# Hybrid mLSTM / MLA / PEER layer: the dots' second operand in PSUM, two product banks, and every second u block split on GpSimd

## Chip, cores and metric

One core of one Trainium2 chip runs the whole layer. The metric is the device time of one execution in microseconds (us). The kernel before takes 1566.36 us, the median of 3 runs (1564.87 to 1568.07).

## The reference, cut to what matters

S = 512 tokens, D = 1024. A mixer (mLSTM heads and latent attention) comes first, then a normalisation, then the sparse block, PEER, which this change is about:

```python
def peer(h, w_q, keys_1, keys_2, u_table, v_table):   # tables: 16384 experts x 1024
    def block(xb):                                    # 128 tokens
        qry = (xb @ w_q).reshape(TB, PEER_HEADS, PEER_D_KEY)
        s1 = jnp.einsum('thd,nd->thn', qry[..., :half], keys_1)
        s2 = jnp.einsum('thd,nd->thn', qry[..., half:], keys_2)
        v1, i1 = lax.top_k(s1, K)
        v2, i2 = lax.top_k(s2, K)
        cand = (v1[..., :, None] + v2[..., None, :]).reshape(TB, PEER_HEADS, K * K)
        sc, ci = lax.top_k(cand, K)                   # 8 heads x 16 experts per token
        idx = ...                                     # expert numbers, from i1, i2, ci
        gate = jax.nn.softmax(sc.astype(jnp.float32), axis=-1)
        act = jax.nn.gelu(jnp.einsum('thed,td->the', u_table[idx], xb), approximate=False)
        return jnp.einsum('the,thed->td', gate * act, v_table[idx])
```

`h2` below is the normalised input of this block. All is float32.

## The kernel before, in words

The 512 tokens are four blocks of 128. The sparse block treats them in two ways.

**Tokens 128 to 511** go through all experts densely. The u table is 128 blocks of 128 experts. For block n SyncE loads `u_raw` (512 KB, ring of four), ScalarE rounds it to `u_hi` (`round_u`, L897), somebody forms `u_lo = u_raw - u_hi` (the *split*), and TensorE makes `z` in 24 matmuls (`first_product`, L1808): eight of `u_hi` with `h2_hi`, eight of `u_hi` with `h2_lo`, eight of `u_lo` with `h2_hi`. I call each eight a pass. Only the third pass waits for the split. ScalarE then takes z out of PSUM through Gelu (`gelu`, L928), and SyncE saves it. z of block n lies in bank n mod 4, so block n waits for the Gelu of block n - 4. ScalarE's order is `round_u(n + 3)`, then `gelu(n)`.

The splits of blocks 0 to 11 are GpSimd's (`split_u`, L656), all others VectorE's (`split_u`, L1408). SyncE's load of block n + 4 waits for the split of block n.

**Tokens 0 to 127** are treated sparsely: for each of 128 slots (8 heads x 16) GpSimd gathers one u row per token (`gather_u`, L665, an indirect DMA of 512 KB into one of 8, later 4, buffers `u_rows`), and VectorE multiplies the row with `h2_nat[:, 0, :]` and sums (`dot`, L1417). The gather into a buffer waits for the dot that last used it. Experts for these tokens come from `choose(0)`, which VectorE runs before any of its splits; the other three `choose(t)` run in pieces between splits, each with 16 pieces of the sizes in `CHOOSE_SIZES` (ns).

The stages of the u blocks are: *pre*, blocks 0 to 71; *main*, blocks 72 to 119, in which TensorE also makes two batches of gate matrices per block (L1855) from `one_hots` of VectorE (L1470); *post*, blocks 120 to 127. Then comes the second phase, the product with the v table (L1884 to L1886).

VectorE's order in pre is written out by a small planner: for each n from 10 it issues `split_u(n + 2)` and then work until the sum of sizes has reached 2800 per block; work is the pieces, with a dot behind each piece over 1500, and dots alone when the pieces are done:

```python
            work, done = rest(), 0
            for n in range(POOL_SPLITS - 2, PRE):
                split_u(n + 2)
                while done < (n - POOL_SPLITS + 3) * SLOT_SIZE:
                    done += next(work, SLOT_SIZE)
```

66 dots stand in pre, 54 in main, 8 in post. In main the order for a block is split, two `one_hots`, one or two dots.

Of the kernel before, what the change touches and what calls it, by code (L numbers as in the profile page):

```python
# [11 lines left out]
ALU = mybir.AluOpType  # L12
ACT = mybir.ActivationFunctionType
# [66 lines left out]
RING = 4  # L80
# [5 lines left out]
POST = PRE + MAIN_BODY * MAIN_TRIPS  # L86
POOL_SPLITS = 12
LEAD = 3
# [5 lines left out]
NORM_AT, TAB_AT = 62, 68  # L94
DOTS_PRE = 66
DOTS_MAIN = [1, 1, 1, 1, 1, 1, 1, 2]
DOTS_POST = [2] * 4
assert DOTS_PRE + MAIN_TRIPS * sum(DOTS_MAIN) + sum(DOTS_POST) == SLOTS


DOT_SIZE, SLOT_SIZE = 1170, 2800
CHOOSE_SIZES = (400, 2000, 1000, 3100, 1000, 1900, 600, 3350, 3350, 3350, 3350, 3350, 3350, 200, 400, 700)
# [66 lines left out]
def build(nc, a):  # L169
    ctx = ExitStack()  # L170
    with ctx:
# [5 lines left out]
        def sem(name):  # L177
            return ctx.enter_context(nc.semaphore(name))
# [124 lines left out]


        act_d = nc.dram_tensor("act_scratch", [E_BLOCKS, P, ND], F32).ap()
        gate_d = nc.dram_tensor("gate_scratch", [CHUNKS, NK, NK, CHUNK], F32).ap()
# [86 lines left out]
        vg_in = [sem(f"vg_in{i}") for i in range(V_ROWS)]  # L393
        dot_done = sem("dot_done")
        z0_ready = sem("z0_ready")
        acc_done = sem("acc_done")
# [23 lines left out]

        def wait_ulo(eng, n, pool=False):

            if pool or isinstance(n, int) and n < POOL_SPLITS:
                eng.wait_ge(ulo_pool, n + 1)
            else:
                eng.wait_ge(ulo_dve, n + (1 - POOL_SPLITS))

# [9 lines left out]
        def _(sp):  # L437
# [59 lines left out]

            def pre(i, pool=False):
                for j in range(PRE_BODY):
                    n = i * PRE_BODY + j  # L500
                    wait_ulo(sp, n, pool)
                    load_u(n + 4, j)
                    if not (isinstance(n, int) and n < 2):
                        save_act(n - 2, j + 2)

            for i in range(POOL_SPLITS // PRE_BODY):
                pre(i, True)
            with sp.Fori(POOL_SPLITS // PRE_BODY, PRE_TRIPS) as i:
                pre(i)
# [7 lines left out]
            def main(i):  # L517
                for j in range(MAIN_BODY):
                    n = i * MAIN_BODY + (PRE + j)
                    wait_ulo(sp, n)  # L520
                    load_u(n + 4, j)
                    save_act(n - 2, j + 2)
                    if j == MAIN_BODY // 2 + 1:
                        save_gates(i, 0)
                    if j == 1 and not (isinstance(i, int) and i == 0):
                        save_gates(i - 1, 1)
# [19 lines left out]
            def post_load_u(n):  # L546

                wait_ulo(sp, n)
                load_u(n + 4, n % 4)
# [63 lines left out]
        def _(pool):  # L613
# [58 lines left out]

            for n in range(POOL_SPLITS):
                split_u(n)
            pool.wait_ge(idx_ready, 1)
            for s in range(SLOTS):
                gather_u(s)

            v_flat = a["v"].rearrange("n p d -> (n p) d")
# [17 lines left out]
        def _(act):  # L697
# [227 lines left out]
            for n in range(1, LEAD):  # L925
                round_u(n, n, True)

            def gelu(n, j, first=False):  # L928
                act.wait_ge(z_done, n + 1)
                if not first:  # L930

                    act.wait_ge(act_saved[j % RING], (n - j % RING) * (16 // RING))
                nc.scalar.activation(act_out[:, j % RING, :], ps[:, j % RING, 0:ND], ACT.Gelu).then_inc(act_ready, 1)  # L933

# [81 lines left out]
        def _(dve):  # L1016
# [400 lines left out]
            def dot():  # L1417

                n = dots[0]
                dots[0] += 1  # L1420
                dve.wait_ge(ug_in[U_SLOT[n]], U_NTH[n] * 16 + 16)
                rows = u_rows[U_SLOT[n]]
                nc.vector.tensor_tensor_reduce(rows[:], rows[:], h2_nat[:, 0, :], 1.0, 0.0, ALU.mult, ALU.add,  # L1423
                                               z0[:, n:n + 1]).then_inc(dot_done, 1)
# [13 lines left out]
            for _ in choose(0):  # L1438
                pass
            def rest():  # L1440

                for t in range(1, TB):
                    made = choose(t)
                    for size in CHOOSE_SIZES:
                        if next(made, 0) is None:
                            yield size
                        if size > 1500 and dots[0] < DOTS_PRE:
                            dot()
                            yield DOT_SIZE
                while dots[0] < DOTS_PRE:  # L1450
                    dot()
                    yield DOT_SIZE

            work, done = rest(), 0
            for n in range(POOL_SPLITS - 2, PRE):
                split_u(n + 2)
                while done < (n - POOL_SPLITS + 3) * SLOT_SIZE:
                    done += next(work, SLOT_SIZE)
                if n == NORM_AT:
                    normalise()  # L1460
                if n == TAB_AT:
                    for t in range(TB - 1):
                        dve.wait_ge(triT_done, t + 1)
                        step(nc.vector.tensor_copy(tab[:, :, t * P:(t + 1) * P],
                                                   ps[:, 4 + t, 0:3 * P].rearrange("p (w t) -> p w t", w=3)))
            for _ in work:
                pass
            settle()
# [16 lines left out]
            for i in range(MAIN_TRIPS):  # L1485
                for j in range(MAIN_BODY):
                    split_u(PRE + i * MAIN_BODY + j + 2)
                    for n in range(2):
                        if i * MAIN_BATCHES + 2 * j + 2 + n < BATCHES:
                            one_hots(i * MAIN_BATCHES + 2 * j + 2 + n)  # L1490
                    for _ in range(DOTS_MAIN[j]):
                        dot()

# [22 lines left out]
            def post_dots(n):  # L1516

                for _ in range(DOTS_POST[n - POST]):
                    dot()
# [62 lines left out]
        def _(pe):  # L1582
# [224 lines left out]

            def first_product(n, j, pool=False, ring=4, first=False, between=()):  # L1808

                pe.wait_ge(uhi_ready, n + 1)  # L1810
                if not first:

                    pe.wait_ge(act_ready, n - (RING - 1))
                o, q = ps[:, j % RING, 0:ND], j % ring
                for m in range(PER_BLOCK):
                    x, k = divmod(m, KD)
                    u, h2 = ((u_hi, h2_hi), (u_hi, h2_lo), (u_lo, h2_hi))[x]
                    if m == 2 * KD:
                        wait_ulo(pe, n, pool)
                    last = mm(o, u[:, q, k, :], h2[:, k, T0:], start=m == 0, stop=m == PER_BLOCK - 1)  # L1820
                    if m == PER_BLOCK - 1:
                        last.then_inc(z_done, 1)
                    for at_m, make in between:
                        if at_m == m:
                            make()

            assert RING <= INDEX[("s12", PH - 1, 0)] % 8
            for j in range(PRE_BODY):

                emptied(pe, JOBS[(len(JOBS) - 1) // 8 * 8 + j][0])  # L1830
                first_product(j, j, True, first=True)
            for n in range(PRE_BODY, POOL_SPLITS):
                first_product(n, n, True)
            with pe.Fori(POOL_SPLITS // PRE_BODY, TRI_TRIP) as i:
                for j in range(PRE_BODY):
                    first_product(i * PRE_BODY + j, j)
            for n in range(TRI_TRIP * PRE_BODY, PRE):
                if n == (TRI_TRIP + 1) * PRE_BODY - 2:

                    pe.wait_ge(tri_ready, 2 * (TB - 1) + 1)  # L1840
                    for t in range(TB - 1):
                        for w in range(3):
                            last = nc.tensor.transpose(ps[:, 4 + t, w * P:(w + 1) * P], tri[:, t, w, :], ident)
                        last.then_inc(triT_done, 1)
                first_product(n, n)

# [11 lines left out]
            def main(i, first=False):  # L1858
                for j in range(MAIN_BODY):
                    between = [((b + 1) * PER_BATCH - 1 - j * PER_BLOCK,  # L1860
                                lambda b=b: gate_matrices(i * MAIN_BATCHES + b, b, first and b < 4))
                               for b in BATCHES_IN[j]]
                    first_product(i * MAIN_BODY + (PRE + j), j, between=between)

# [3 lines left out]
            for n in range(POST, E_BLOCKS):  # L1868
                first_product(n, n, ring=2)

# [89 lines left out]
```

## Time and profile before

| | |
|---|---|
| median of 3 runs | 1566.36 us (1564.87 to 1568.07) |
| the profiled execution: its own time | 1567.12 us |
| its span, first to last instruction | 1565.3 us |
| u blocks, from the first matmul to the last | 395.2 to 1029.5 us |
| of these: pre, main, post | to 704, to 990, to 1029.5 us |
| busy share of the span: TensorE, VectorE, ScalarE, GpSimd | 97%, 78%, 39%, 35% |
| mean granted TensorE clock | 0.988 |

The profile lists instructions by engine (PE is TensorE, DVE VectorE, ACT ScalarE, POOL GpSimd, SP SyncE) with start and duration in us. A bracket at the end of a row, as [3.76 <-DVE u_lo L1412], is the time for which the engine sat idle before that instruction and whose work released it. Successive VectorE instructions overlap a little, so the distance of their starts is what one costs: a dot whose row says 1.23 is followed by the next instruction 1.15 us after its start, and a split counts about as much.

### The profile page before, as it was taken

What the parts mean: (1) busy time and instruction counts of PE and PEld (TensorE: products, weight loads), DVE (VectorE), ACT (ScalarE), POOL (GpSimd) and SP (SyncE); (2) the same over time, 40 slices, a digit from 0 to 9 for tenths busy, and PEclk for the clock granted to TensorE, in tenths of its full rate; (3) what the DMA queues carried; (4) which work ended last, traced back from release to release, by engine and by line L of the source; (5) the groups of instructions that cost most, each with busy time, mean ns of one, the idle gap of its engine ahead of it and who ended that gap; (6) DMA issues with size and microseconds to landing.
All of it is one profiled execution on the core that took longest, in us unless ns stands there. A gap on an engine that the chain in (4) does not pass through costs nothing.

```text
span 1565.3 us, 22972 instructions
## 1 busy us (share of the span) xinstructions
PE 1515.6 (97%) x8069; PEld 1354.6 (87%) x8069; DVE 1222.7 (78%) x2336; ACT 613.3 (39%) x816; POOL 549.8 (35%) x297
## 2 busy tenths in 40 slices
PE   6999989999989999999999999979999999999999
PEld 6879658788989999999999999968888888888887
DVE  4537463288989999989999999638878788787886
ACT  4363442222423333335666565433233232332321
POOL 2213231232643222762333323314434434344341
PEclk9999989999999999999999999989999999999999
DMA  5400201221467877997888888989999999999993
GB/s 198 142 28 1 108 8 60 85 78 68 160 226 267 274 261 258 367 413 285 291 331 314 283 331 311 357 315 370 354 353 356 350 358 351 352 357 351 354 354 127
DMA packets 181667, 399.37 MB, mean 255 GB/s; under 512 B 12260, under 2 KB 111844, under 8 KB 180072
## 3 DMA queue, kind: packets, MB, share of 16 engines
q1 hardware_dynamic: 144744, 264.41, 48.1%
q0 software_dynamic: 36864, 134.23, 23.4%
q8 instruction: 30, 0.49, 0.1%
q14 instruction: 29, 0.24, 0.0%
HBM read 346.16 MB, written 52.43 MB: 255 GB/s over the span
## 4 chain that ended last, share of the span: by engine, by line
PE 83%; DVE 7%; DMA 3%; POOL 3%; ACT 1%; issue 1%; SPq 1%; DVEq 0%; ACTq 0%
PE banks L1820 24%; PE banks L1613 15%; PE banks L1884 11%; PE banks L1886 11%; PE banks L1885 11%; PE banks L1855 5%; POOL u_rows L669 3%; DMA u_rows<-in_u,idx 1%; DMA v_raw<-in_v 1%; PE banks L1801 1%; DMA u_raw<-in_uT 1%; PE banks L1664 1%; DVE wo_lo L1241 1%; PE banks L1723 1%; SPq L570 1%
## 5 line engine op out<-in xcount | busy, mean ns | idle before, releaser
L669 POOL DMA_INDIRECT u_rows<-in_u,idx x128 | 205.3, 1604 | 360.6 <-DVE z L1423 334.2
L691 POOL DMA_INDIRECT v_rows<-in_v,idx x128 | 205.5, 1606 | 334.7 <-DVE x_res L1550 295.3
L1884 PE MATMUL banks<-v_hi,w_hi 128*128 128x512 f32 x768 | 299.6, 390 | 7.7 <-DVE v_lo L1497 7.7
L1885 PE MATMUL banks<-v_lo,w_hi 128*128 128x512 f32 x768 | 299.5, 390 | 0.0
L1886 PE MATMUL banks<-v_hi,w_lo 128*128 128x512 f32 x768 | 299.3, 390 | 0.0
L982 ACT ACTIVATE v_hi<-v_raw 128x1024 fp32r<-128x1024 f32 x128 | 125.8, 1049 | 339.5 <-PE banks L1886 320.4
L1497 DVE TENSOR_TENSOR v_lo<-v_raw,v_hi 128x1024 fp32r<-128x1024 f32 x128 | 153.5, 1220 | 121.5 <-ACT v_hi L982 121.5
L1820 PE MATMUL banks<-h_lo,u_hi 128*128 128x384 f32 x1024 | 210.1, 338 | 0.0
L1820 PE MATMUL banks<-h_hi,u_lo 128*128 128x384 f32 x1024 | 201.1, 338 | 8.7 <-DVE u_lo L1412 8.7
L1820 PE MATMUL banks<-h_hi,u_hi 128*128 128x384 f32 x1024 | 203.9, 340 | 0.0
L1820 PEld LDWEIGHTS banks<-h_hi,u_lo 128*128 128x128 f32 x1024 | 181.3, 190 | 10.0 <-DVE u_lo L1412 10.0
L1820 PEld LDWEIGHTS banks<-h_hi,u_hi 128*128 128x128 f32 x1024 | 177.8, 190 | 0.3 <-ACT u_hi L909 0.3
L1820 PEld LDWEIGHTS banks<-h_lo,u_hi 128*128 128x128 f32 x1024 | 177.6, 188 | 0.0
L1884 PEld LDWEIGHTS banks<-v_hi,w_hi 128*128 128x128 f32 x768 | 144.5, 188 | 38.1 <-issue 8.1
L1885 PEld LDWEIGHTS banks<-v_lo,w_hi 128*128 128x128 f32 x768 | 144.6, 188 | 30.2
L1886 PEld LDWEIGHTS banks<-v_hi,w_lo 128*128 128x128 f32 x768 | 144.6, 188 | 30.0
L1550 DVE SCALAR_TENSOR_TENSOR x_res<-v_rows,w,x_res 128x1024 f32<-128x1024 f32 x128 | 163.5, 1278 | 0.9
L1423 DVE CUSTOM_DVE_ANT_0 u_rows<-u_rows,h_nat 128x1024 f32<-128x1024 f32 x128 | 154.1, 1219 | 9.3 <-DMA u_rows<-in_u,idx 9.2
L903 ACT ACTIVATE u_hi<-u_raw 128x1024 fp32r<-128x1024 f32 x122 | 128.8, 1057 | 60.0 <-PE banks L1820 44.4
L1412 DVE TENSOR_TENSOR u_lo<-u_raw,u_hi 128x1024 fp32r<-128x1024 f32 x116 | 140.9, 1218 | 12.6 <-ACT u_hi L909 8.6
L933 ACT ACTIVATE act_out<-banks 128x384 f32<-128x384 f32 x128 | 62.1, 485 | 192.6 <-PE banks L1820 178.6
L960 ACT ACTIVATE stage<-banks 128x512 f32<-128x512 f32 x96 | 109.2, 1137 | 68.3 <-PE banks L1855 68.3
(256 smaller groups left out, 1971.9 us busy)
## 6 DMA issues: line engine op xcount, KB each, us to landing
u_raw<-in_uT SPq DMA_DIRECT2D x128, 512.0 KB
v_raw<-in_v SPq DMA_DIRECT2D x128, 512.0 KB, 6.1
act_scratch<-act_out SPq DMA_DIRECT2D x128, 192.0 KB
act_in<-act_scratch SPq DMA_DIRECT2D x32, 768.0 KB, 7.6
gates<-gate_scratch SPq DMA_DIRECT2D x32, 768.0 KB, 12.8
gate_scratch<-stage SPq DMA_DIRECT2D x11, 2048.0 KB
wi_raw<-in_w_in SPq DMA_DIRECT2D x8, 1024.0 KB, 8.7
wq_raw<-in_w_q SPq DMA_DIRECT2D x8, 1024.0 KB, 5.4
```

What stands on the lines that cost most here:

```text
L669: nc.gpsimd.indirect_dma_start(u_rows[U_SLOT[s]][:], None, a["u"], bass.IndirectOffsetOnAxis(ap=idx0[:, s:s + 1], axis=0)).then_inc(ug_in[ ...
L691: nc.gpsimd.indirect_dma_start(v_rows[s % V_ROWS][:], None, v_flat, bass.IndirectOffsetOnAxis(ap=idx0[:, s:s + 1], axis=0)).then_inc(vg_in ...
L903: nc.scalar.activation(u_hi[:, j % 4, :, :], u_raw[:, j % 4, :, :], ACT.Copy).then_inc(uhi_ready, 1)
L1412: nc.vector.tensor_tensor(u_lo[:, slot, :, :], u_raw[:, n % 4, :, :], u_hi[:, slot, :, :].bitcast(F32), ALU.subtract).then_inc(ulo_dve, 1)
L1423: nc.vector.tensor_tensor_reduce(rows[:], rows[:], h2_nat[:, 0, :], 1.0, 0.0, ALU.mult, ALU.add, z0[:, n:n + 1]).then_inc(dot_done, 1)
L1497: nc.vector.tensor_tensor(v_lo[q][:, j, :], v_raw[:, j, :], v_hi[q][:, j, :].bitcast(F32), ALU.subtract).then_inc(vlo_ready, 1)
L1550: nc.vector.scalar_tensor_tensor(out=x_res[:, 0, :], in0=v_rows[n % V_ROWS][:], scalar=w0[:, n:n + 1], in1=x_res[:, 0, :], op0=ALU.mult, o ...
L1613: last = mm(o, lhs(x, k), rhs(y, k), start=n == k == 0, stop=n == 2 and k == KD - 1)
L1820: last = mm(o, u[:, q, k, :], h2[:, k, T0:], start=m == 0, stop=m == PER_BLOCK - 1)
L1884: mm(y, w, v_hi[q][:, j, ds], start=first and j == 0, stop=False)
L1885: mm(y, w, v_lo[q][:, j, ds], start=False, stop=False)
L1886: end = mm(y, w_lo[q][:, j, t * P:(t + 1) * P], v_hi[q][:, j, ds], start=False, stop=last and j == GROUP - 1)
```

## The change

- ScalarE copies `h2_nat[:, 0, :]` into PSUM banks 2 and 3 (`h2_first`) before the first Gelu, once those banks are free. The dots read it there; the first dot waits for the copy (`h2_placed`).
- z has two banks instead of four, 0 and 1 (`Z_BANKS`). Block n now waits for the Gelu of block n - 2.
- Of the blocks 16 to 119 the even ones, 52 in all (`SHARED`), are split by GpSimd. VectorE only increments `share_open` in that place and then does two dots. Blocks 12 to 15 and the odd ones stay with VectorE.
- GpSimd's order becomes one merged list of gathers and splits: at each place n the gathers whose buffers' dots stand before n, then, if n + 2 is shared, a wait for `share_open` and the split.
- VectorE's order in pre: split or `share_open`, the dots of `DOTS_AT[n]`, and then pieces until their sizes sum to 2150 per block, with no dots in this sum. The first two dots now stand at n = 14 where one stood at n = 10. The numbers of dots per stage stay 66, 54 and 8; in main the dots stand ahead of the `one_hots`.

```diff
-POOL_SPLITS = 12
+POOL_FIRST, SHARE_FROM = 12, 16
+Z_BANKS = 2
...
-DOTS_PRE = 66
-DOTS_MAIN = [1, 1, 1, 1, 1, 1, 1, 2]
-DOTS_POST = [2] * 4
...
+SHARED = list(range(SHARE_FROM, POST, 2))
+DOTS_AT = [2 if n + 2 in SHARED else 0 for n in range(POST)] + [2] * 4 + [0] * 4
+for _n in [*range(PRE - 17, PRE, 2)][:8] + [*range(PRE + 5, POST, 6)]:
+    DOTS_AT[_n] += 1
...
-DOT_SIZE, SLOT_SIZE = 1170, 2800
+PIECE_SIZE = 2150
...
+        h2_first = ps[:, 2:4, :].rearrange("p b d -> p (b d)")
...
-            for n in range(POOL_SPLITS):
+            for n in range(POOL_FIRST):
                 split_u(n)
             pool.wait_ge(idx_ready, 1)
-            for s in range(SLOTS):
+            s = 0
+            for n in range(len(DOTS_AT)):
+                while s < SLOTS and (U_BEFORE[s] is None or U_BEFORE[s] < sum(DOTS_AT[:n])):
+                    gather_u(s)
+                    s += 1
+                if n + 2 in SHARED:
+
+                    pool.wait_ge(share_open, SHARED.index(n + 2) + 1)
+                    split_u(n + 2)
+            while s < SLOTS:
                 gather_u(s)
+                s += 1
...
+            for j in (2, 3):
+                emptied(act, JOBS[(len(JOBS) - 1) // 8 * 8 + j][0])
+            nc.scalar.activation(h2_first, h2_nat[:, 0, :], ACT.Copy).then_inc(h2_placed, 1)
...
-                nc.scalar.activation(act_out[:, j % RING, :], ps[:, j % RING, 0:ND], ACT.Gelu).then_inc(act_ready, 1)
+                nc.scalar.activation(act_out[:, j % RING, :], ps[:, j % Z_BANKS, 0:ND], ACT.Gelu).then_inc(act_ready, 1)
...
-                nc.vector.tensor_tensor_reduce(rows[:], rows[:], h2_nat[:, 0, :], 1.0, 0.0, ALU.mult, ALU.add,
+                nc.vector.tensor_tensor_reduce(rows[:], rows[:], h2_first, 1.0, 0.0, ALU.mult, ALU.add,
...
+            def splits_and_dots(n):
+
+                if n + 2 in SHARED:
+                    dve.sem_inc(share_open, 1)
+                else:
+                    split_u(n + 2)
+                for _ in range(DOTS_AT[n]):
                     dot()
...
+            work, done = itertools.chain(*(choose(t) for t in range(1, TB))), 0
+            sizes = itertools.cycle(CHOOSE_SIZES)
+            for n in range(POOL_FIRST - 2, PRE):
+                splits_and_dots(n)
+                while done < (n - POOL_FIRST + 3) * PIECE_SIZE:
+                    done += next(sizes)
+                    next(work, None)
...
-                    split_u(PRE + i * MAIN_BODY + j + 2)
+                    splits_and_dots(PRE + i * MAIN_BODY + j)
...
-                    for _ in range(DOTS_MAIN[j]):
-                        dot()
...
-                    pe.wait_ge(act_ready, n - (RING - 1))
-                o, q = ps[:, j % RING, 0:ND], j % ring
+                    pe.wait_ge(act_ready, n - (Z_BANKS - 1))
+                o, q = ps[:, j % Z_BANKS, 0:ND], j % ring
```

The waits for a finished split (`wait_ulo`) now count on two semaphores, GpSimd's for shared blocks and VectorE's for the others.

## Rows read from the trace of the kernel before

**Rows 1.** Busy time in stretches: PE, PEld, DVE, ACT, POOL (x instructions), clock, DMA share, GB/s.
```profile
395.00:448.00 53.00, 53.00 (x308) 52.83 (x307) 51.49 (x172) 19.78 (x27) 30.72 (x11) 1.00 0.45 147
448.00:472.00 24.00, 19.00 (x93) 18.53 (x93) 18.78 (x96) 6.07 (x8) 12.19 (x11) 0.86 0.92 342
472.00:704.00 232.00, 232.00 (x1344) 231.97 (x1343) 221.92 (x389) 83.51 (x114) 97.14 (x59) 1.00 0.87 306
704.00:990.00 286.00, 285.34 (x1918) 285.02 (x1917) 278.04 (x643) 171.70 (x191) 92.76 (x57) 1.00 0.85 305
990.00:1030.00 40.00, 36.27 (x200) 35.23 (x199) 23.68 (x25) 15.87 (x21) 7.50 (x5) 0.96 0.95 352
```

**Rows 2.** TensorE's waits over the whole span: us in total, times, longest.
```profile
PE banks L1820 <- DVE u_lo L1412: 8.7, 4, 3.8
...
PE banks L1855 <- DVE gate_rows L1480: 0.7, 1, 0.7
```

**Rows 3.** Timeline of all engines, 446 to 467: start, us, engine, instruction.
```profile
448.12 1.22 DVE L1412 TENSOR_TENSOR u_lo<-u_raw,u_hi 128x1024 fp32r<-128x1024 f32 x1
449.39 1.66 PE L1820 MATMUL banks<-h_hi,u_lo 128*128 128x384 f32 x8 [1.24 <-DVE u_lo L1412]
...
452.28 1.55 PE L1820 MATMUL banks<-h_lo,u_hi 128*128 128x384 f32 x8
...
455.16 1.23 DVE L1423 CUSTOM_DVE_ANT_0 u_rows<-u_rows,h_nat 128x1024 f32<-128x1024 f32 x1 [3.61 <-DMA u_rows<-in_u,idx]
...
456.31 1.22 DVE L1412 TENSOR_TENSOR u_lo<-u_raw,u_hi 128x1024 fp32r<-128x1024 f32 x1
...
457.59 2.93 PE L1820 MATMUL banks<-h_hi,u_lo 128*128 128x384 f32 x8 [3.76 <-DVE u_lo L1412]
457.71 0.35 SPq L482 DMA_DIRECT2D u_raw<-in_uT  x1
...
458.75 0.94 POOL L669 DMA_INDIRECT u_rows<-in_u,idx  x1 [0.30 <-issue]
...
460.31 2.76 PE L1820 MATMUL banks<-h_hi,u_hi 128*128 128x384 f32 x8
...
464.99 1.06 ACT L903 ACTIVATE u_hi<-u_raw 128x1024 fp32r<-128x1024 f32 x1 [3.95 <-DMA u_raw<-in_uT]
...
465.85 1.37 PE L1820 MATMUL banks<-h_hi,u_hi 128*128 128x384 f32 x7
466.04 0.49 ACT L933 ACTIVATE act_out<-banks 128x384 f32<-128x384 f32 x1
```

**Rows 4.** GpSimd's splits: ns min/median/max, then first and last start.
```profile
L662 POOL TENSOR_TENSOR u_lo<-u_raw,u_hi x12: 2387/2391/5643, 381.7 to 430.5; 128x1024 fp32r<-128x1024 f32 x12
```

**Rows 5.** Timeline, 424 to 436.
```profile
426.13 9.98 POOL L662 TENSOR_TENSOR u_lo<-u_raw,u_hi 128x1024 fp32r<-128x1024 f32 x2 [1.77 <-ACT u_hi L903]
428.27 5.58 DVE L1385 TENSOR_TENSOR picked<-picked,pay 128x3200 f32<-128x3200 f32 x1
433.89 3.49 DVE L1388 TENSOR_REDUCE e_f<-picked 128x64 f32<-128x3200 f32 x1
```

**Rows 6.** Timeline, 265 to 268.
```profile
265.78 4.61 POOL L653 TENSOR_TENSOR wq_lo<-wq_raw,wq_hi 128x2048 fp32r<-128x2048 f32 x1 [46.34 <-ACT wq_hi L707]
...
266.84 0.69 DVE L1300 TENSOR_TENSOR x_res<-x_res,banks 128x512 f32<-128x512 f32 x1 [0.96 <-PE banks L1613]
```

**Rows 7.** Timeline, 490 to 497.
```profile
491.05 3.48 DVE L1380 TENSOR_TENSOR picked<-sc_f,iota_c 128x3200 f32<-128x3200 f32 x1
491.40 3.95 POOL L669 DMA_INDIRECT u_rows<-in_u,idx  x1 [5.12 <-DVE z L1423]
```

**Rows 8.** VectorE's last dot of the pre stage, timeline 700 to 707.
```profile
702.80 1.23 DVE L1423 CUSTOM_DVE_ANT_0 u_rows<-u_rows,h_nat 128x1024 f32<-128x1024 f32 x1 [0.76 <-DMA u_rows<-in_u,idx]
```

**Rows 9.** The post stage, timeline 1015 to 1024.
```profile
1016.42 2.93 PE L1820 MATMUL banks<-h_hi,u_lo 128*128 128x384 f32 x8 [2.33 <-DVE u_lo L1412]
1018.05 1.06 ACT L909 ACTIVATE u_hi<-u_raw 128x1024 fp32r<-128x1024 f32 x1 [7.47 <-DMA u_raw<-in_uT]
...
1023.84 0.44 PE L1820 MATMUL banks<-h_hi,u_lo 128*128 128x384 f32 x1 [1.39 <-DVE u_lo L1412]
```

More of the change, by code:

```diff
@@ L94 @@
 NORM_AT, TAB_AT = 62, 68
-DOTS_PRE = 66
-DOTS_MAIN = [1, 1, 1, 1, 1, 1, 1, 2]
-DOTS_POST = [2] * 4
-assert DOTS_PRE + MAIN_TRIPS * sum(DOTS_MAIN) + sum(DOTS_POST) == SLOTS
-DOT_SIZE, SLOT_SIZE = 1170, 2800
+SHARED = list(range(SHARE_FROM, POST, 2))
+DOTS_AT = [2 if n + 2 in SHARED else 0 for n in range(POST)] + [2] * 4 + [0] * 4
+for _n in [*range(PRE - 17, PRE, 2)][:8] + [*range(PRE + 5, POST, 6)]:
+    DOTS_AT[_n] += 1
+DOTS_PRE = sum(DOTS_AT[:PRE])
+assert sum(DOTS_AT) == SLOTS
+PIECE_SIZE = 2150
 CHOOSE_SIZES = (400, 2000, 1000, 3100, 1000, 1900, 600, 3350, 3350, 3350, 3350, 3350, 3350, 200, 400, 700)
@@ L394, in build @@
         dot_done = sem("dot_done")
+        h2_placed = sem("h2_placed")
+        share_open = sem("share_open")
         z0_ready = sem("z0_ready")
@@ L419, in u_slot, with wait_ulo @@
             return n % 4 if n < POST else n % 2
-        def wait_ulo(eng, n, pool=False):
-            if pool or isinstance(n, int) and n < POOL_SPLITS:
-                eng.wait_ge(ulo_pool, n + 1)
+        def wait_ulo(eng, i, base, body):
+            if isinstance(i, int):
+                n = i * body + base
+                if n < POOL_FIRST:
+                    eng.wait_ge(ulo_pool, n + 1)
+                elif n < SHARE_FROM:
+                    eng.wait_ge(ulo_dve, n + 1 - POOL_FIRST)
+                elif n in SHARED:
+                    eng.wait_ge(ulo_pool, POOL_FIRST + SHARED.index(n) + 1)
+                else:
+                    eng.wait_ge(ulo_dve, n + 1 - POOL_FIRST - sum(m < n for m in SHARED))
+            elif base % 2 == 0:
+                eng.wait_ge(ulo_pool, i * (body // 2) + (POOL_FIRST + (base - SHARE_FROM) // 2 + 1))
             else:
-                eng.wait_ge(ulo_dve, n + (1 - POOL_SPLITS))
+                eng.wait_ge(ulo_dve, i * (body // 2) + (SHARE_FROM - POOL_FIRST + (base - SHARE_FROM - 1) // 2 + 1))
         def staged_at(b):
@@ L496, in save_act, with pre @@
                              act_out[:, j % RING, :]).then_inc(act_saved[j % RING], 16)
-            def pre(i, pool=False):
+            def pre(i):
                 for j in range(PRE_BODY):
                     n = i * PRE_BODY + j
-                    wait_ulo(sp, n, pool)
+                    wait_ulo(sp, i, j, PRE_BODY)
                     load_u(n + 4, j)
@@ L504, in pre @@
                         save_act(n - 2, j + 2)
-            for i in range(POOL_SPLITS // PRE_BODY):
-                pre(i, True)
-            with sp.Fori(POOL_SPLITS // PRE_BODY, PRE_TRIPS) as i:
+            for i in range(SHARE_FROM // PRE_BODY):
+                pre(i)
+            with sp.Fori(SHARE_FROM // PRE_BODY, PRE_TRIPS) as i:
                 pre(i)
@@ L519, in main @@
                     n = i * MAIN_BODY + (PRE + j)
-                    wait_ulo(sp, n)
+                    wait_ulo(sp, i, PRE + j, MAIN_BODY)
                     load_u(n + 4, j)
@@ L546, in post_load_u @@
             def post_load_u(n):
-                wait_ulo(sp, n)
+                wait_ulo(sp, 0, n, 1)
                 load_u(n + 4, n % 4)
@@ L1420, in dot @@
                 dots[0] += 1
+                if n == 0:
+                    dve.wait_ge(h2_placed, 1)
                 dve.wait_ge(ug_in[U_SLOT[n]], U_NTH[n] * 16 + 16)
                 rows = u_rows[U_SLOT[n]]
-                nc.vector.tensor_tensor_reduce(rows[:], rows[:], h2_nat[:, 0, :], 1.0, 0.0, ALU.mult, ALU.add,
+                nc.vector.tensor_tensor_reduce(rows[:], rows[:], h2_first, 1.0, 0.0, ALU.mult, ALU.add,
                                                z0[:, n:n + 1]).then_inc(dot_done, 1)
@@ L1439, in _ @@
                 pass
[L1440 to L1447, printed above, removed]
-                            dot()
-                            yield DOT_SIZE
-                while dots[0] < DOTS_PRE:
-                    dot()
[L1452 to L1458, printed above, removed]
+            def splits_and_dots(n):
+                if n + 2 in SHARED:
+                    dve.sem_inc(share_open, 1)
+                else:
+                    split_u(n + 2)
+                for _ in range(DOTS_AT[n]):
+                    dot()
+            work, done = itertools.chain(*(choose(t) for t in range(1, TB))), 0
[5 more added lines that the diff above has]
+                    next(work, None)
                 if n == NORM_AT:
@@ L1465, in _ @@
                                                    ps[:, 4 + t, 0:3 * P].rearrange("p (w t) -> p w t", w=3)))
-            for _ in work:
-                pass
+            assert next(work, 0) == 0
             settle()
@@ L1490, in _ @@
                             one_hots(i * MAIN_BATCHES + 2 * j + 2 + n)
-                    for _ in range(DOTS_MAIN[j]):
-                        dot()
             def split_v(g, q, j):
@@ L1516, in post_dots @@
             def post_dots(n):
-                for _ in range(DOTS_POST[n - POST]):
+                for _ in range(DOTS_AT[n]):
                     dot()
@@ L1805, in _, with first_product @@
                     queries(h + 1, 1)
-            def first_product(n, j, pool=False, ring=4, first=False, between=()):
+            def first_product(n, j, i, base, body, ring=4, first=False, between=()):
                 pe.wait_ge(uhi_ready, n + 1)
                 if not first:
-                    pe.wait_ge(act_ready, n - (RING - 1))
-                o, q = ps[:, j % RING, 0:ND], j % ring
+                    pe.wait_ge(act_ready, n - (Z_BANKS - 1))
+                o, q = ps[:, j % Z_BANKS, 0:ND], j % ring
                 for m in range(PER_BLOCK):
@@ L1818, in first_product @@
                     if m == 2 * KD:
-                        wait_ulo(pe, n, pool)
+                        wait_ulo(pe, i, base, body)
                     last = mm(o, u[:, q, k, :], h2[:, k, T0:], start=m == 0, stop=m == PER_BLOCK - 1)
@@ L1827, in _ @@
             assert RING <= INDEX[("s12", PH - 1, 0)] % 8
[L1828 to L1834, printed above, removed]
+            for n in range(SHARE_FROM):
+                if n < Z_BANKS:
+                    emptied(pe, JOBS[(len(JOBS) - 1) // 8 * 8 + n][0])
+                first_product(n, n, 0, n, 1, first=n < Z_BANKS)
+            with pe.Fori(SHARE_FROM // PRE_BODY, TRI_TRIP) as i:
                 for j in range(PRE_BODY):
-                    first_product(i * PRE_BODY + j, j)
+                    first_product(i * PRE_BODY + j, j, i, j, PRE_BODY)
             for n in range(TRI_TRIP * PRE_BODY, PRE):
@@ L1844, in _ @@
                         last.then_inc(triT_done, 1)
-                first_product(n, n)
+                first_product(n, n, 0, n, 1)
             def gate_matrices(n, b, first=False):
@@ L1862, in main @@
                                for b in BATCHES_IN[j]]
-                    first_product(i * MAIN_BODY + (PRE + j), j, between=between)
+                    first_product(i * MAIN_BODY + (PRE + j), j, i, PRE + j, MAIN_BODY, between=between)
             main(0, True)
@@ L1868, in _ @@
             for n in range(POST, E_BLOCKS):
-                first_product(n, n, ring=2)
+                first_product(n, n, 0, n, 1, ring=2)
             def second(g, q, first=False, last=False):
```

## The prediction, made before the changed kernel ran

> **What bounds the kernel now.** The page's busy shares name TensorE, so I went to the stretches first. In the u blocks TensorE is busy all of 395 to 448, all of 472 to 704 and 285.34 of 286 us to 990, at full clock; VectorE is nearly full there too, 221.92 of 232 and 278.04 of 286 [rows 1]. Taking work off VectorE gives nothing by itself in these stretches. A gain can only come from where TensorE sits idle or runs slowly: 448 to 472 (19.00 of 24 us busy, clock 0.86) and 990 to 1030 (36.27 of 40) [rows 1]. The list of waits agrees: 8.7 us in four waits for VectorE's `u_lo`, 0.7 us in one for `gate_rows` [rows 2].
>
> Then the timeline at 448. VectorE, which has only then finished `choose(0)`, splits block 12 at 448.12, and the third pass of block 12 starts at 449.39 after 1.24 us idle. The third pass of block 13 starts only at 457.59, after 3.76 us idle. Between the two splits stands the first dot, which sits 3.61 us for its gathered row and starts at 455.16; the split of block 13 follows at 456.31 [rows 3]. The gap has a price behind it: the pass at 457.59 lasts to 460.31, and the next has 2.76 against 1.55 for a normal one [rows 3], with the stretch's clock at 0.86 [rows 1]. So for a few us after the gap the clock was at its lower level, 1.2 GHz. The 1.24 us gap had no such effect.
>
> **The change, part by part.**
>
> *The first dot leaves its place ahead of the split of block 13*; it stands at n = 14 in place of n = 10. A block of 24 matmuls takes 232 x 24 / 1344 = 4.14 us at full clock [rows 1]; since a few records are missing I take 4.16, and 1.387 for a pass. From 452.28, the second pass of block 13, five passes lead to the first pass of block 15: 459.2. It was seen at 465.85 [rows 3]. So 6.6 us are lost here, 3.76 idle, the rest clock.
>
> Is the split of 13 early enough now? After the split of 12 (448.12, 1.14) come pieces named 400 and 2000; the one named 3350 takes 3.48 [rows 7], so I add 4%: 2.5. The next split runs 451.7 to 452.9 and is wanted at 452.28 + 1.39 = 453.7.
>
> *The blocks behind it.* Block n's third pass is wanted at 453.7 + 4.16 (n - 13). I step VectorE through its new list, 1.15 for a dot and 1.14 for a split (455.16 to 456.31 [rows 3]), and GpSimd's split at 2.39 [rows 4]:
> - 14: pieces 1000 and 3100, split done 457.9, wanted 457.8: 0 to 0.3 late.
> - 15: done 459, wanted 462.0.
> - 16 (GpSimd): pieces 1000, 1900, opened 461.6, done 464.1, wanted 466.2.
> - 17: two dots, 600, 3350; done 469.2, wanted 470.3.
> - 18: opened 469.2, done 471.7, wanted 474.5.
> - 20: two dots, 3350, split of 19, 3350; opened 479.6, done 482.0, wanted 482.8.
> - 22, 23: 1.5 and 1.2 early.
>
> Per pair VectorE has 1.14 + 2.30 + 4.3 x 1.04 = 7.9 us of work for 8.3 us of TensorE, so the lead grows, and by n = 54 the pieces have run out. New stalls: nothing at least, and at the narrow places 14, 17 and 20 up to 1.5 us together. I take 0.8, the middle, since nothing says which.
>
> *What makes GpSimd late.* Eight gathers stand before its first shared split. The last began at 458.75 [rows 3]; now two more splits beside them may hold them about 0.8 each: free at 460 to 461.5, just ahead of 461.6. Behind its wait for `share_open` only later gathers are queued, with eight buffers, so four pairs, in hand.
>
> *GpSimd beside VectorE.* At 426 the two take turns: two splits on GpSimd need 9.98 us in place of 4.8, and VectorE's two-input piece 5.58 in place of 3.48, while the reduction behind it, with one input, keeps 3.49 beside the end of them [rows 5, 7]. So a GpSimd split that falls on a split, a two-input piece or a `one_hots` is paid for by VectorE. Does it under two dots with one operand in PSUM? The nearest row: `x_res + bank` took 0.69 us in the middle of a GpSimd subtraction of 4.61, and neither grew [rows 6]. Bounds: nothing, or the whole 2.39 per pair; I take nothing, by that row. Two dots last 2.30 and the split 2.39, so 0.1 to 0.3 us per pair stick out, within its 0.4 of slack. Gathers gain: 0.94 alone [rows 3], 3.95 beside a two-input piece [rows 7].
>
> [...]
>
> *Main.* 286 / 48 = 5.96 us a block for TensorE; VectorE's busy 278.04 [rows 1] loses 24 splits of 1.14, 27 us. TensorE stays the bound: nothing. The 0.7 us on `gate_rows` [rows 2] came from VectorE being held in its last pre dot until 704, the row being late at 702.80 [rows 8]. With the dots spread, it is early: 0.7 won.
>
> *Two z banks.* Block n + 2 waits for `gelu(n)`, which has a block's time but stands behind `round_u(n + 3)` and its load. The load may be 2 x 4.16 - 0.6 - 1.06 - 0.49 = 6.2 us late for ScalarE before TensorE feels it (0.6 for ScalarE's own start). The longest such wait was 3.95, for a load issued at 457.71 and used at 464.99, amid the gathers [rows 3]. These now meet four loads, not two. 0 to 1 us, inside the 0.8. In main ScalarE has 171.70 of 286 [rows 1], so a Gelu is never a block late.
>
> *h2 into PSUM.* One ScalarE copy of 128x1024, near 1.06 us [rows 3]; ScalarE is busy 19.78 of 53 there [rows 1], and block 2 needs `gelu(0)` only 8 us after the first product starts. Nothing; 1 us if the banks come late.
>
> *Post.* The waits of 2.33 and 1.39 [rows 9] come from VectorE's order, which stays. But the second also hangs on a load 7.47 us late [rows 9]. By the new list two gathers that stood just ahead of post go out a block or more earlier: 1 MB, 3 us at 352 GB/s [rows 1]. Gain 0 to 1.7; I take 0.5.
>
> **Sum.** -6.6 - 0.7 - 0.5 + 0.8 = -7.0. The profiled execution took 1567.12 (span 1565.3), so 1560.1; on the median of 1566.36, which lies 0.8 lower, 1559.4.
>
> **Rivals.**
> - *Forecast* (0.68): 1556.5 to 1562.5.
> - *The gap moves* (0.18). GpSimd's split of 16 or 20, or the split of 17, comes 3 us late and the clock falls again for 2.9. For: leads of 0.8 to 1.1 us, DMA at 0.92 there [rows 1]. Against: the steps above close. Of the 7.8 won 5.9 are lost: 1564.5, up to 1567.
> - *The dots still shut GpSimd out* (0.08), on the other side. A pair then costs VectorE 2.4 more, 10.3 for 8.3 us; it decides from 0.4 a pair on. 22 pairs with pieces, 2.0 each: +44 - 7, about 1603. Against: [rows 6].
> - *Two banks hold TensorE back* (0.06): loads over 6.2 us late in ten blocks, 1 us each: +10 - 7, 1569.5.
>
> **Chances.** 0.2%, or 3.1 us, is about what a measurement of this kernel can tell from no change. Faster: the forecast and a little of the second case, 0.70. Same: 0.17. Slower: 0.13, the last two. Low end of the range: no new loss, the post gain whole, 0.8 of scatter: 1556.5. High end, into the second case: 1566.
>
> **What would show it.** TensorE's wait at block 13 gone and the clock 1.00 from 448 to 472; first dots near 462; GpSimd splits of about 2.39 under two dots; no wait on `gate_rows`; TensorE's pace from 472 to 990 unchanged. I am wrong if TensorE waits over 2 us for a `u_lo` or an `act_out` between 455 and 490, or if GpSimd's shared splits take 3.5 us and more.

## The result, and the profile after

The changed kernel takes **1570.56 us** (median of 12 runs, 1568.63 to 1574.6), the kernel before 1566.22 in the same rounds (12 runs, 1564.87 to 1569.61): a ratio of **1.0028, 95% interval 1.0020 to 1.0036**. It is slower, by 4.3 us, where 7 us less were forecast and the range ended at 1566.0. The profiled execution took 1570.04, with a span of 1568.2 against 1565.3.

The stretches of the changed kernel, in the columns of [rows 1]:

```profile
395.00:448.00 53.00, 53.00 (x308) 52.85 (x307) 51.50 (x172) 20.85 (x28) 30.81 (x11) 1.00 0.44 147
448.00:472.00 24.00, 22.76 (x131) 22.47 (x131) 23.86 (x99) 6.37 (x9) 20.74 (x13) 1.00 0.91 348
472.00:704.00 232.00, 230.59 (x1336) 230.12 (x1335) 209.79 (x383) 87.35 (x115) 159.80 (x90) 1.00 0.89 318
704.00:990.00 286.00, 278.44 (x1859) 275.48 (x1858) 286.00 (x587) 167.09 (x186) 125.13 (x73) 1.00 0.82 293
990.00:1030.00 40.00, 35.86 (x210) 34.93 (x209) 25.19 (x30) 17.10 (x22) 8.88 (x7) 1.00 1.00 360
```

The first two rows are what was forecast: TensorE goes from 19.00 to 22.76 busy us in 448 to 472, and its granted clock from 0.86 to 1.00. The fourth is not. From 704 to 990 VectorE was busy 278.04 us [rows 1] and had 24 splits taken from it, yet it is busy all of the 286 us, with 587 instructions in place of 643, and TensorE drops to 278.44. The bound has changed engines. TensorE's waits, in the columns of [rows 2], from 448 on:

```profile
PE banks L1881 <- DVE gate_rows L1509: 7.6, 5, 1.8
PE banks L1847 <- DVE u_lo L1443: 6.2, 4, 2.3
...
PE banks L1847 <- ACT act_out L964: 0.6, 1, 0.6
```

The list shows 7.6 us for `gate_rows` where 0.7 stood [rows 2]. To place the time I read from the timeline where TensorE starts the first pass of blocks 12, 16, 72, 73, 120 and 127, and its first wait for a `v_lo` (in ordinary numbers, us):

```
                          before   after   after - before   forecast
start to block 12         445.21  445.23       +0.02
blocks 12 to 16            24.80   18.24       -6.56          -6.6
blocks 16 to 72           233.94  235.75       +1.81          +0.8
block 72 (first gates)      6.82    5.86       -0.96          -0.7
blocks 73 to 120          279.50  289.48       +9.98           0
blocks 120 to 127          35.07   34.19       -0.88  } together
127 to the v_lo wait       28.37   27.90       -0.47  } -0.5
```

The differences add up to +2.9, the difference of the spans. Without the row of blocks 73 to 120 they add up to -7.0, which is the sum of the prediction. That they meet it so closely is partly luck: blocks 16 to 72 lost 1.0 us more than forecast, and the gates and the end won 1.1 more. The row of blocks 73 to 120 is the large miss.

The early part by itself, in the columns of [rows 3]:

```profile
451.50 1.21 DVE L1443 TENSOR_TENSOR u_lo<-u_raw,u_hi 128x1024 fp32r<-128x1024 f32 x1
...
453.68 1.55 PE L1847 MATMUL banks<-h_hi,u_lo 128*128 128x384 f32 x8
...
459.31 1.55 PE L1847 MATMUL banks<-h_hi,u_hi 128*128 128x384 f32 x8
...
460.95 2.43 POOL L679 TENSOR_TENSOR u_lo<-u_raw,u_hi 128x1024 fp32r<-128x1024 f32 x1
461.29 1.20 DVE L1456 CUSTOM_DVE_ANT_0 u_rows<-u_rows,banks 128x1024 f32<-128x1024 f32 x1
```

Block 13 is split at 451.50 and its third pass starts at 453.68 with no wait, against 457.59 after 3.76 idle [rows 3]. Block 15's first pass is at 459.31 (forecast 459.2) instead of 465.85 [rows 3]. The first dots come at 461.29, and here GpSimd's split (460.95) does lie beside them; the dot keeps its 1.20 us and the split its 2.43.

Now the stretch that went wrong, VectorE and GpSimd from 805 to 824:

```profile
804.69 0.68 DVE L1505 TENSOR_TENSOR oh<-consts,tab 128x512 f32<-128x512 f32 x1
805.04 1.15 POOL L686 DMA_INDIRECT u_rows<-in_u,idx  x1 [4.39 <-DVE z L1456]
805.30 3.93 DVE L1509 TENSOR_SCALAR gate_rows<-consts,tab 128x128 f32<-128x128 f32 x4
...
806.21 2.41 POOL L679 TENSOR_TENSOR u_lo<-u_raw,u_hi 128x1024 fp32r<-128x1024 f32 x1
...
809.28 1.16 PE L1881 MATMUL banks<-gate_rows,oh 128*128 128x128 f32 x8 [0.78 <-DVE gate_rows L1509]
809.75 1.10 DVE L1509 TENSOR_SCALAR gate_rows<-consts,tab 128x128 f32<-128x128 f32 x4
...
810.78 1.21 DVE L1456 CUSTOM_DVE_ANT_0 u_rows<-u_rows,banks 128x1024 f32<-128x1024 f32 x1
...
816.29 4.09 POOL L679 TENSOR_TENSOR u_lo<-u_raw,u_hi 128x1024 fp32r<-128x1024 f32 x1 [1.73 <-DVEq L1476]
816.32 1.21 DVE L1443 TENSOR_TENSOR u_lo<-u_raw,u_hi 128x1024 fp32r<-128x1024 f32 x1
...
818.06 3.18 DVE L1509 TENSOR_SCALAR gate_rows<-consts,tab 128x128 f32<-128x128 f32 x4
...
822.78 1.21 DVE L1456 CUSTOM_DVE_ANT_0 u_rows<-u_rows,banks 128x1024 f32<-128x1024 f32 x1
```

Four `gate_rows` take 1.10 us alone and 3.93 and 3.18 beside a GpSimd split. The splits run at 806.21 and 816.29; the dots that should cover them run at 810.78 and 822.78, 4.6 and 6.5 us later. What released the second split is named `DVEq`: VectorE's queue, at the line of `share_open`, and no instruction of VectorE's. That line from 800 to 824 (count, ns, first and last start):

```profile
L1476 DVEq EVENT_SEMAPHORE  x2: 21/21/21, 803.7 to 816.2; - x2
```

So the two increments went out 7.1 and 6.6 us before the first of their dots, while the two batches of one-hots that stand ahead of those dots, ten instructions, were still to run. The second split started at once; the first was held until 806.21 by a gather of GpSimd's own (805.04). The groups of 704 to 990 add it up (mean ns of one, then idle before and its releasers):

```profile
L1509 DVE TENSOR_SCALAR gate_rows<-consts,tab 128x128 f32<-128x128 f32 x368 | 152.6, 480 | 0.0
...
L679 POOL TENSOR_TENSOR u_lo<-u_raw,u_hi 128x1024 fp32r<-128x1024 f32 x22 | 73.5, 3340 | 31.7 <-DVEq L1476 18.3 <-ACT u_hi L930 13.3
```

A `gate_rows` costs 480 ns; before the change the same group shows 342. Over 368 of them that is 51 us, against the 27 us that 24 splits freed. The chain of 800 to 830 says the same, nearly all of it VectorE's:

```profile
by line: DVE gate_rows L1509 49.4%; DVE oh L1505 20.1%; DVE u_rows L1456 15.3%; DVE u_lo L1443 11.9%; issue 4.0%; DVE z L1456 0.4%
```

### The profile page after: what moved, and what is told of

It is laid out like the page before. It is cut to its first block, busy times and chain, and to the rows that moved or that the text cites. A ratio compares the mean times of both kernels' runs of the same rounds, so it can differ in the third digit from the quotient of the medians.

```text
span 1568.2 us, 23044 instructions
## 1 busy us (share of the span) xinstructions
PE 1514.2 (97%) x8069; PEld 1349.7 (86%) x8069; DVE 1227.0 (78%) x2284; ACT 615.6 (39%) x817; POOL 655.1 (42%) x349
## 4 chain that ended last, share of the span: by engine, by line
PE 62%; DVE 33%; issue 2%; DMA 1%; ACT 1%; SPq 0%; DVEq 0%; ACTq 0%
PE banks L1640 15%; PE banks L1910 11%; PE banks L1912 11%; PE banks L1911 11%; DVE gate_rows L1509 9%; PE banks L1847 8%; DVE u_rows L1456 5%; DVE oh L1505 3%; DVE u_lo L1443 3%; DVE picked L1411 2%; DVE picked L1416 2%; DVE e_f L1419 2%; DMA v_raw<-in_v 1%; PE banks L1828 1%; PE banks L1881 1%
## 5 line engine op out<-in xcount | busy, mean ns | idle before, releaser
L686 POOL DMA_INDIRECT u_rows<-in_u,idx x128 | 153.4, 1199 | 201.2 <-DVE z L1456 167.0
L679 POOL TENSOR_TENSOR u_lo<-u_raw,u_hi 128x1024 fp32r<-128x1024 f32 x64 | 190.8, 2983 | 85.2 <-ACT u_hi L930 54.7
L1509 DVE TENSOR_SCALAR gate_rows<-consts,tab 128x128 f32<-128x128 f32 x384 | 157.0, 475 | 0.0
L1456 DVE CUSTOM_DVE_ANT_0 u_rows<-u_rows,banks 128x1024 f32<-128x1024 f32 x128 | 150.4, 1211 | 0.2 <-DVE tri L1434 0.2
```

The source lines that it names most:

```text
L679: nc.gpsimd.tensor_tensor(u_lo[:, n % 4, :, :], u_raw[:, n % 4, :, :], u_hi[:, n % 4, :, :].bitcast(F32), ALU.subtract).then_inc(ulo_pool, 1)
L686: nc.gpsimd.indirect_dma_start(u_rows[U_SLOT[s]][:], None, a["u"], bass.IndirectOffsetOnAxis(ap=idx0[:, s:s + 1], axis=0)).then_inc(ug_in[ ...
L1456: nc.vector.tensor_tensor_reduce(rows[:], rows[:], h2_first, 1.0, 0.0, ALU.mult, ALU.add, z0[:, n:n + 1]).then_inc(dot_done, 1)
L1509: nc.vector.tensor_scalar(gate_rows[:, slot, w, :], iota, tab[:, 1, t:t + 1], tab[:, 0, t:t + 1], ALU.is_equal, ALU.mult).then_inc(oh_read ...
```

## The experiments

**Theory A:** `dve.sem_inc(share_open, 1)` is carried out when VectorE's queue reaches it, while the work queued ahead of it is still to be done; so the split lies under the one-hots, which it blocks, and not under the dots. **Theory B:** the dots with h2 in PSUM still shut GpSimd out. **Theory C:** two z banks hold TensorE back. Besides, one part of the change was done alone. Each kernel was timed beside the kernel before (1565.9 to 1566.6 in its rounds).

### 1. own_wait: the release waits for VectorE's own work

```diff
+            def drained():
+                settle()
+                dve.wait_ge(ulo_dve, dve_splits[0])
+                if dots[0]:
+                    dve.wait_ge(dot_done, dots[0])
+                if made_hots[0]:
+                    dve.wait_ge(oh_ready, made_hots[0] * (BATCH + 1))
...
                 if n + 2 in SHARED:
+                    drained()
                     dve.sem_inc(share_open, 1)
```

The two new counters, whose lines are left out here, count the splits and batches of one-hots that VectorE has been given so far.

> The changed kernel, but VectorE waits for the end of all its own instructions before it releases GpSimd's split. Theory A (the release leaves VectorE's queue before the work ahead of it is done, so the split lies under the one-hots and not under the two dots): the split now starts with the first dot, four gate_rows take 1.1 us again instead of 3 to 4, VectorE is again some 30 us short of filling the middle stretch, and the time is 1558 to 1561 us. Theory B (dots with h2 in PSUM shut GpSimd out as those with h2 in SBUF did): the split starts under the dots but lasts over 4 us, or the dots do, VectorE stays full in the middle stretch, 1568 us or more. Theory C (two z banks hold TensorE back, not the split): 1568 to 1572 us, with full-speed gate_rows.

1557.21 us (5 runs, 1555.28 to 1559.57), ratio 0.9948, interval 0.9935 to 0.9961; just under the 1558 at which theory A's range began. The increment for these dots goes out at 811.5, 0.2 us before the first, and the split now begins with that dot:

```profile
810.28 1.11 DVE L1523 TENSOR_SCALAR gate_rows<-consts,tab 128x128 f32<-128x128 f32 x4
...
811.65 2.40 POOL L679 TENSOR_TENSOR u_lo<-u_raw,u_hi 128x1024 fp32r<-128x1024 f32 x1 [6.43 <-DVEq L1489]
811.70 1.22 DVE L1468 CUSTOM_DVE_ANT_0 u_rows<-u_rows,banks 128x1024 f32<-128x1024 f32 x1 [0.31 <-DVE gate_rows L1523]
```

```profile
704.00:990.00 286.00, 286.00 (x1919) 286.00 (x1919) 244.25 (x589) 169.17 (x189) 121.13 (x76) 1.00 0.83 304
```

Four `gate_rows` take 1.11 us, a split 2.40, a dot 1.22: none pays for the other. VectorE falls to 244.25 of 286 and TensorE is busy throughout. Blocks 73 to 120 take 279.49 us, to 0.01 those of the kernel before, and the 1.8 us lost in blocks 16 to 72 are gone as well (233.98). VectorE's own wait costs it 0.31 us here. (Of this profile's span, 1555.4, another 0.9 us were won ahead of block 12, where nothing is changed.) Theory A holds; B and C fall, since both dots in PSUM and two banks are still there.

### 2. share_pre_only: sharing only up to block 71

```diff
-SHARED = list(range(SHARE_FROM, POST, 2))
+SHARED = list(range(SHARE_FROM, PRE, 2))
```

The places of the dots stay; `wait_ulo` counts VectorE's splits from block 72 on.

> The changed kernel, but GpSimd shares the u splits only up to block 71; VectorE makes all those from block 72 on. Theory A: in the middle stretch nothing of GpSimd's runs beside the gate_rows, so TensorE is the bound there as before the change, and the time is 1558 to 1562 us. Theory B gives the same. Theory C: 1568 to 1572 us, since the two banks are still there.

1559.90 us (5 runs), ratio 0.9960, interval 0.9947 to 0.9973. Blocks 73 to 120 take 279.49 us; 235.72 for 16 to 72, as in the changed kernel. So the 10 us come from the splits shared in the middle stretch. The 1.8 us come from ahead of it, and own_wait has shown them to hang on the early release too.

### 3. first_dots_later: one edit to the kernel before

```diff
@@ rest(): a dot between two pieces
-                        if size > 1500 and dots[0] < DOTS_PRE:
+                        if size > 1500 and dots[0] < DOTS_PRE and slot_now[0] >= 13:
```

`slot_now` is the n of the loop that issues the splits.

> The kernel before, with one edit: no dot is issued before the split of block 15. If the wait of 3.8 us for the split of block 13 goes and nothing takes its place: 1566.2 less 4 to 7, so 1559.5 to 1562 us. If the wait only moves to a later block: 1564.5 to 1566.5 us.

1563.78 us (12 runs), ratio 0.9982, interval 0.9974 to 0.9991: a smaller gain than the first case expected, and between the two. Blocks 12 to 16 take 18.39 us, so the gap at block 13 is gone. But blocks 16 to 72 take 235.38 (+1.4) and block 72 takes 8.12 (+1.3). The first of these:

```profile
463.17 3.48 DVE L1380 TENSOR_TENSOR picked<-sc_f,iota_c 128x3200 f32<-128x3200 f32 x1
466.02 1.06 ACT L903 ACTIVATE u_hi<-u_raw 128x1024 fp32r<-128x1024 f32 x1 [2.82 <-DMA u_raw<-in_uT]
466.57 2.35 DVE L1412 TENSOR_TENSOR u_lo<-u_raw,u_hi 128x1024 fp32r<-128x1024 f32 x2
...
467.84 1.68 PE L1822 MATMUL banks<-h_hi,u_lo 128*128 128x384 f32 x8 [1.12 <-DVE u_lo L1412]
```

The split of block 16 stands behind a 3.48 us piece, and TensorE waits 1.12 us for it. In the changed kernel GpSimd does that split. The second is the wait on `gate_rows` at the start of the middle stretch, 2.0 us in place of 0.7 [rows 2], with the dots still packed ahead of it. So moving the first dot is worth 6.4 us where it stands; to keep them the list behind it must have room, which the changed list gives. No run has its evenly spread dots without the sharing, so which of the two makes the room, and whether blocks 16 to 71 need the sharing at all, isn't shown.

### 4. two_banks: the kernel before with two z banks

```diff
+Z_BANKS = 2
-                    pe.wait_ge(act_ready, n - (RING - 1))
-                o, q = ps[:, j % RING, 0:ND], j % ring
+                    pe.wait_ge(act_ready, n - (Z_BANKS - 1))
+                o, q = ps[:, j % Z_BANKS, 0:ND], j % ring
```

and the same index in `gelu`; only the first two blocks now skip the wait.

> The kernel before, with two z banks in place of four and nothing else. Theories A and B: TensorE's waits for act_out stay under 1 us in sum, 1566 to 1567 us. Theory C: 1570 us and more, with TensorE waiting for act_out at many blocks.

1565.59 us (11 runs), ratio 0.9999, interval 0.9990 to 1.0007: no difference. TensorE waits for no `act_out`, and blocks 73 to 120 take 279.49 us.

### 5. own_wait_sbuf: own_wait with h2 in SBUF

```diff
-                nc.vector.tensor_tensor_reduce(rows[:], rows[:], h2_first, 1.0, 0.0, ALU.mult, ALU.add,
+                nc.vector.tensor_tensor_reduce(rows[:], rows[:], h2_nat[:, 0, :], 1.0, 0.0, ALU.mult, ALU.add,
```

> The kernel of own_wait (VectorE waits for its own work before it releases GpSimd's split), but the dots read h2 from SBUF, as before the change. If the operand in PSUM is what lets the split and the two dots run side by side: the split, or the dots, take 2.4 us longer a pair, VectorE goes from 244 busy us of 286 in the middle stretch to 300 and more, so it is the bound there, and the time is 1568 to 1580 us. If it makes no difference where h2 lies: 1556 to 1559 us, with splits of 2.4 us under dots of 1.15 us.

1616.87 us (5 runs), ratio 1.0329, interval 1.0315 to 1.0344; 60 us over own_wait, far beyond what was expected.

```profile
804.19 1.21 DVE L1468 CUSTOM_DVE_ANT_0 u_rows<-u_rows,h_nat 128x1024 f32<-128x1024 f32 x1
...
808.94 2.39 POOL L679 TENSOR_TENSOR u_lo<-u_raw,u_hi 128x1024 fp32r<-128x1024 f32 x1 [2.11 <-DVEq L1489]
808.99 3.42 DVE L1468 CUSTOM_DVE_ANT_0 u_rows<-u_rows,h_nat 128x1024 f32<-128x1024 f32 x1 [0.31 <-DVE gate_rows L1523]
```

The same dot takes 1.21 us alone and 3.42 beside the split, which keeps its 2.39: VectorE stands still for nearly the whole of it. I expected 2.4 us a pair in the middle stretch, and about 2.2 came (3.42 - 1.21; dots at 2122 ns in the mean, blocks 73 to 120 in 300.13 us, +20.6), but I had left out the pieces of blocks 16 to 72, where VectorE has less slack: 269.74 us, +35.8. In this list of work, sharing pays only with the operand in PSUM.

### 6. no_release: no `share_open`

```diff
                 if n + 2 in SHARED:
-                    dve.sem_inc(share_open, 1)
+                    pass
```

with GpSimd's wait for it left out as well.

> The changed kernel without the semaphore that releases GpSimd's split: it starts when u_hi is there and the gathers ahead of it are out. If the release in the changed kernel holds nothing back because VectorE's queue gives it well ahead of the work, this is within 3 us of the changed kernel: 1567 to 1574 us, with gate_rows groups of 3 to 4 us as there. If the release still shields VectorE by a good part, the time is over 1575 us.

1577.27 us (5 runs), ratio 1.0076, interval 1.0063 to 1.0090: over the 1575 of the second expectation, and 6.7 us over the changed kernel. Even the early release shields VectorE in part: blocks 73 to 120 take 296.94 us without it, 289.48 with it, 279.49 with one that waits. The price on each `gate_rows` hardly moves (491 ns against 480); TensorE waits for them 12.7 us in 11 waits in place of 7.6 in 5. Why it waits so much more often stays open.

### 7. every_fourth: the early release, half the shared splits

```diff
-SHARED = list(range(SHARE_FROM, POST, 2))
+SHARED = list(range(SHARE_FROM, PRE, 2)) + list(range(PRE, POST, 4))
```

> The changed kernel with its early release, but in the middle stretch GpSimd takes every fourth block in place of every second (12 splits, not 24). Two blocks with a shared split cost VectorE some 12.5 us there, two without one 11.1, against TensorE's 11.9. If the sum decides, the mean of 11.8 is just under TensorE's time and the loss of 10 us in the middle stretch goes nearly whole: 1559 to 1562 us. If each early split costs TensorE time of its own: half the loss stays, 1564 to 1566 us.

1560.33 us (5 runs), ratio 0.9965, interval 0.9951 to 0.9979.

```profile
704.00:990.00 286.00, 286.00 (x1920) 286.00 (x1919) 277.80 (x604) 170.86 (x191) 87.66 (x65) 1.00 0.83 303
```

The same stretch by groups:

```profile
L1513 DVE TENSOR_SCALAR gate_rows<-consts,tab 128x128 f32<-128x128 f32 x368 | 128.3, 419 | 0.0
```

`gate_rows` still pays (419 ns), VectorE has 277.80 us of work in 286, and TensorE loses nothing: 279.49 us. Halving the number of early splits took away all of the loss. An early split costs TensorE nothing by itself; the loss begins where VectorE's work for two blocks passes TensorE's 11.89 us.

### 8. own_wait_pre_only: edits 1 and 2 together

> Both edits together: VectorE waits for its own work before it releases GpSimd's split, and GpSimd shares splits only up to block 71. If sharing in the middle stretch is worth nothing, because TensorE is the bound there with or without it: 1556 to 1558.5 us, as own_wait, with 11.9 us for two blocks of the middle stretch. If VectorE's free time there is worth something: 1559 us or more.

1557.68 us (5 runs), ratio 0.9945, interval 0.9932 to 0.9959: as own_wait. In the middle stretch VectorE is busy 265.87 of 286 us here and 244.25 there, with the same 279.49 us for blocks 73 to 120. Sharing there buys nothing, even when it is done right.

### 9. own_wait_post: a try at the next wait

```diff
             post_dots(POST + 3)
+            split_u(POST + 5)
             for k in range(2, 4):
                 split_v(0, 0, k)
             dve.wait_ge(dot_done, SLOTS)
             weights(0, 0, True)
-            split_u(POST + 5)
```

> The kernel of own_wait, with the split of block 125 ahead of two v splits and the first weights product on VectorE in place of behind them. TensorE's wait of 2.3 us for that split near the end of the u blocks should go: 1557.2 less 1 to 2.5, so 1554.7 to 1556.2 us; if the v stretch waits for its weights in its place, 1557 us.

1557.68 us (5 runs), ratio 0.9946, interval 0.9933 to 0.9960: no gain over own_wait. The wait for that split is gone, and another stands in its place:

```profile
1009.91 2.32 PE L1861 MATMUL banks<-h_hi,u_hi 128*128 128x384 f32 x8 [2.42 <-ACT act_out L964]
```

The Gelu of two blocks earlier stood behind a `u_hi` on ScalarE that had waited 5.74 us for its load. Here a z bank was short; in the changed kernel that cost 0.6 us, in own_wait_sbuf 2.6. Whether four banks would have given the 2 us was not tried, since the dots need banks 2 and 3.

## Why the prediction was wrong

- **The failed step** is that GpSimd's split lies under the two dots, at which the prediction counted only "0.1 to 0.3 us per pair" sticking out. It rested on where `share_open` stands in VectorE's list. In the trace the increments went out 7.1 and 6.6 us before the dots that follow them in the list, and the splits lay under `gate_rows`. The prediction did say that a split on a `one_hots` is paid for by VectorE, but counted none there. That price (3.93 - 1.10 = 2.8 and 3.18 - 1.10 = 2.1 us a pair on `gate_rows`) was in no term of the sum. It is shown: own_wait changes only when the increment goes out (VectorE waits 0.31 us for it), and all of the loss goes.
- **The step that hung on it**, "TensorE stays the bound: nothing" for the middle stretch, was +9.98 us. Each pair saved VectorE 1.1 us of split and cost it 2.1 to 2.8. Once VectorE was full, two blocks took 12.5 us ((988.62 - 813.17) / 14 pairs, from the starts of first passes) against 11.89. The first pairs were still hidden: up to 806 the pace was TensorE's. Behind that nearly all of the loss sits in every third pair (13.8 to 13.9 us, the others 11.9 to 12.1), the rhythm in which VectorE's list has a third dot.
- **The same cause ahead of it**: +1.8 us in blocks 16 to 72, where 0 to 1.5 had been taken for other reasons. VectorE's split there lasts 2.53 us beside GpSimd's, and TensorE waits 1.41:

```profile
601.64 2.40 POOL L679 TENSOR_TENSOR u_lo<-u_raw,u_hi 128x1024 fp32r<-128x1024 f32 x1
602.60 2.53 DVE L1443 TENSOR_TENSOR u_lo<-u_raw,u_hi 128x1024 fp32r<-128x1024 f32 x1
...
605.19 1.68 PE L1847 MATMUL banks<-h_hi,u_lo 128*128 128x384 f32 x8 [1.41 <-DVE u_lo L1443]
```

- **Right in mechanism and size**: the first dot's move, -6.6 forecast and -6.56 measured (-6.4 done alone); the dots beside GpSimd's split unhurt with h2 in PSUM, by the reading of [rows 6]; the `gate_rows` wait at the start of the middle stretch (-0.7, measured -0.96); two z banks nothing.
- **The end of the u blocks** was taken at -0.5 and came at -1.35. That stays open: two_banks has -1.2 and -1.0 in the same places with no such gathers moved, so profiles differ there by that much anyway.
- **The rival on the slower side** had the right symptom, GpSimd and VectorE shutting each other out, under the wrong instruction. It laid it on the dots, and own_wait_sbuf shows what that would have been: 1616.9, where 1603 was worked out. The test that the prediction set, shared splits of 3.5 us and more, came true in part: they took 2.38 to 4.85, and 14 of the 52 took 3.5 or more.

The hint was in the code. `dve.sem_inc(x2_ready, 1)` and `dve.sem_inc(freed["D"], 1)` each stand behind a `settle()`, which waits for VectorE's own steps; `share_open` stood behind none. It needed none to be right, only to be at the right time.

The Trainium skill (Perfetto Trace Analysis, Sequencer Loop and DVE / Act Engine Instruction) says that the sequencer pushes an engine's instruction into a queue and is then ready for the next, while that instruction's own semaphore update comes once its bytes are written. The page doesn't name a stand-alone increment, but the trace agrees with what would follow for one, at 7.1 and 6.6 us ahead of the dots. The Trainium skill (SBUF — State Buffer, Who interferes with whom) exempts a VectorE instruction with at most one SBUF input only outside the two-port modes, and lists `tensor_scalar` among those that can enter them. The trace agrees, since `gate_rows`, a `TENSOR_SCALAR` with one tensor read, went from 1.10 to 3.93 us for four.

## What to carry to other kernels

A semaphore raised by an instruction of its own marks what the queue has reached, not what the engine has done (here 6.6 to 7.1 us apart); to make it mark a time, let the engine wait for its own last result first, or hang it on that instruction (not tried here). When work is moved to an engine that shares a path with the one relieved, ask which instructions it will run beside, and add to VectorE's list the price on each of these, not only on those it was meant for. Relieving an engine that isn't the bound buys nothing: 279.49 us for blocks 73 to 120 with VectorE at 244, 266 and 278 busy us of 286, and a loss at once when it passes the bound.

## What the runs showed of the hardware

- A GpSimd subtraction of 128x1024 from SBUF (2.4 us) stops `TENSOR_SCALAR` on VectorE with one tensor read of 128x128 (four: 1.10 to 3.93 us), and a dot with both operands in SBUF (1.21 to 3.42). A dot with one operand in PSUM keeps its 1.22 beside the same subtraction.
- Where one clearly came first, the second comer was blocked: with GpSimd's split at 601.64, VectorE's at 602.60 takes 2.53 and GpSimd's keeps its 2.40. Close starts went either way: 0.03 us apart at 816.3, VectorE's split kept its 1.21 and GpSimd's took 4.09; 0.05 us apart at 808.9 in own_wait_sbuf, the dot took 3.42 and GpSimd's split kept its 2.39.
- A semaphore increment that is an instruction of its own, behind queued VectorE work, went out 7.1 and 6.6 us before the VectorE instruction that follows it in the list.
- VectorE's wait for its own last result costs it 0.31 us ahead of a dot.
- TensorE's pace in blocks 73 to 120 is the same to 0.01 us in eight kernels, while that from block 120 on moves by 1 us from profile to profile of kernels that time alike. So one profile can show a change of 1 us in the first stretch and not in the second.
